# A split-precision decoder trunk: value slabs of the up projections by seven block products, gated products split at the down stage

## The reference, cut to what matters

```python
def conv_ffn(u, w_up, conv_w, conv_b, w_down):
    h = u @ w_up.astype(u.dtype)               # (512,1024) @ (1024,5632)
    h = causal_depthwise_conv(h, conv_w, conv_b)
    gate, val = jnp.split(h, 2, axis=-1)
    return (jax.nn.silu(gate) * val) @ w_down.astype(u.dtype)   # (512,2816) @ (2816,1024)

for i in range(DEPTH):
    ...                                        # mixer of layer i
    f = conv_ffn(rms_norm(x, norm_ffn_pre[i]), ffn_w_up[i], ffn_conv_w[i], ffn_conv_b[i], ffn_w_down[i])
    x = x + rms_norm(f, norm_ffn_post[i])
```

## Time and profile before

| | us |
|---|---|
| median of 3 runs (lowest, highest) | 1138.78 (1138.66, 1138.90) |
| the profiled execution | 1138.84 |
| its span, first to last instruction | 1137.1 |
| granted TensorE clock, mean | 0.999 of full speed |
| busy: TensorE, its weight loads, VectorE, ScalarE, GpSimd | 1127.7, 949.7, 695.5, 524.2, 35.9 |

### The profile page before, as it was taken

The page is one execution under the profiler, slowest core; times in us unless marked ns, Lnnn a source line. Parts: engine busy times, 40 slices in busy tenths (PEclk is TensorE's granted clock), DMA queues, the critical chain, the costliest instruction groups (busy, mean ns, idle before and its releaser), DMA issues.

```text
span 1137.1 us, 14741 instructions
## 1 busy us (share of the span) xinstructions
PE 1127.7 (99%) x5730; PEld 949.7 (84%) x5730; DVE 695.5 (61%) x825; ACT 524.2 (46%) x610; POOL 35.9 (3%) x93
## 2 busy tenths in 40 slices
PE   8999999999999999999999999999999999999998
PEld 7888888888888988888888888899888888888886
DVE  6778889999763865655655321597655565552124
ACT  5667676767533643443443221475443434331213
POOL 6000000000100000000000000000000000000000
PEclk9999999999999999999999999999999999999999
DMA  8244343433233133233233223512232232323221
GB/s 274 76 133 148 121 128 122 133 127 130 75 111 126 61 111 111 79 106 111 74 111 108 98 90 111 167 38 75 93 111 94 91 109 76 110 85 115 96 74 74
DMA packets 85390, 121.74 MB, mean 107 GB/s; under 512 B 4215, under 2 KB 71391, under 8 KB 85344
## 3 DMA queue, kind: packets, MB, share of 16 engines
q1 hardware_dynamic: 85162, 121.02, 32.0%
q10 hardware_dynamic: 182, 0.07, 0.0%
HBM read 118.92 MB, written 2.16 MB: 106 GB/s over the span
## 4 chain that ended last, share of the span: by engine, by line
PE 99%; DMA 1%; ACT 0%; DVE 0%; issue 0%; SPq 0%; DVEq 0%
PE bank L1040 29%; PE bank L307 19%; PE bank L308 19%; PE bank L309 19%; PE bank L515 6%; PE bank L801 1%; PE bank L792 1%; PE bank L753 1%; PE bank L743 1%; PE bank L431 1%; PE bank L1214 1%; DMA raw<-in_ssd_w_in 1%; PE bank L1229 0%; PE bank L1230 0%; PE bank L1231 0%; PE bank L721 0%
## 5 line engine op out<-in xcount | busy, mean ns | idle before, releaser
L307 PE MATMUL bank<-h_hi,w_hi 128*128 128x512 f32 x928 | 364.5, 393 | 0.0
L309 PE MATMUL bank<-h_hi,w_lo 128*128 128x512 f32 x928 | 361.5, 390 | 0.0
L308 PE MATMUL bank<-h_lo,w_hi 128*128 128x512 f32 x928 | 361.2, 389 | 0.0
L277 DVE TENSOR_TENSOR w_lo<-raw,w_hi 128x2048 fp32r<-128x2048 f32 x90 | 206.1, 2289 | 215.0 <-ACT w_hi L272 215.0
L534 DVE SCALAR_TENSOR_TENSOR tmp<-bank,par,tmp 128x511 f32<-128x511 f32 (+2 forms) x248 | 184.9, 747 | 125.3 <-ACT tmp L525 112.4
L272 ACT ACTIVATE w_hi<-raw 128x2048 fp32r<-128x2048 f32 x90 | 171.7, 1908 | 154.0 <-PE bank L1040 152.3
L309 PEld LDWEIGHTS bank<-h_hi,w_lo 128*128 128x128 f32 x928 | 174.2, 188 | 37.1
L307 PEld LDWEIGHTS bank<-h_hi,w_hi 128*128 128x128 f32 x928 | 174.3, 188 | 36.2 <-issue 0.8
L308 PEld LDWEIGHTS bank<-h_lo,w_hi 128*128 128x128 f32 x928 | 174.4, 188 | 35.0
L525 ACT ACTIVATE tmp<-bank,par 128x512 f32<-128x512 f32 x112 | 86.2, 774 | 221.7 <-PE bank L309 201.4
L1040 PE MATMUL bank<-w_lo,act_hi 128*128 128x512 f32 x348 | 107.2, 389 | 0.0
(11 more groups left out here) (203 smaller groups left out, 1030.1 us busy)
## 6 DMA issues: line engine op xcount, KB each, us to landing
raw<-in_ffn_w_up SPq DMA_DIRECT2D x44, 1024.0 KB, 5.0
raw<-in_ffn_w_down SPq DMA_DIRECT2D x22, 1024.0 KB, 4.8
raw<-in_ssd_w_in SPq DMA_DIRECT2D x19, 1024.0 KB, 5.2
decay<-ac_dram SPq DMA_DIRECT2D x16, 512.0 KB, 5.5
raw<-in_ssd_w_out SPq DMA_DIRECT2D x8, 1024.0 KB, 4.8
from_start<-ac_dram SPq DMA_DIRECT2D x32, 128.0 KB, 4.6
xres<-in_x SPq DMA_DIRECT2D x4, 512.0 KB, 6.0
result<-xres SPq DMA_DIRECT2D x3, 512.0 KB, 2.6
```

The source lines that it names most:

```text
L277: dve.tensor_tensor(lo[:], raw[n % 2][:], hi[:].bitcast(F32), ALU.subtract).then_inc(lo_ready, 1)
L307: pe.matmul(dst, wh, xh, start=first, stop=False, **kw)
L308: pe.matmul(dst, wh, xl, start=False, stop=False, **kw)
L309: return pe.matmul(dst, wl, xh, start=False, stop=last, **kw)
```

## The change

The value slabs of passes 2 to 10 of both layers are no longer multiplied as two block products. Slab (1024 x 256) and features (1024 x 512 positions) are cut in two in each direction, and the 2x2 product of these parts is made of seven products of quarters in place of eight (Strassen's scheme in the variant of Winograd): four block weights and seven half-width products of 128 columns by 256 positions, 4 blocks of the contraction x 3 passes each, into halves of banks 0 to 3.

- GpSimd makes, once per layer, the four sums of features (`combos_pool`, ten steps of 128x1024, into `t_new`), which ScalarE and VectorE split into `t_hi`, `t_lo` in pass 1; and in each such pass four sums of weights in place in `raw` (`weights_pool`, four steps of 128x512), which are split by halves into the slot of the pass's own gate slab (`weights_hi_act`, `weights_lo_dve`). The raw slab is released when these are made, not when its own low part is.
- ScalarE copies the first product out of its bank (`first_seven_act`), VectorE assembles the value blocks in `val` in SBUF by four additions (`sevens_dve`); the value taps read `val`.
- The taps and products of the value blocks of pass i are made behind the next value slab's split, at the turn to pass i+1.
- The product gate x value stays in `gated` (float32) and is split two blocks at a time, into `dn_hi`, `dn_lo`, in the down stage; the first pair in pass 4 (`down_hi_act`, `down_lo_dve`).
- The slots of `w_hi`, `w_lo` follow `w_slot`; the first down slab takes chunks 2, 3, 0, 1.
- All loops `Fori` are written out.

```diff
+        def w_slot(n):
+            for l in range(2):
+                i = n - S_UP[l]
+                if 0 <= i < UP_SLABS + DOWN_SLABS:
+                    return (n + max(min(i, UP_SLABS) // 2 - SEVEN0, 0)) % 2
+            return n % 2
-        def load(sp, n, source, view, i=0):
-            if n >= 2:
-                sp.wait_ge(lo_ready, n - 1 + 2 * i)
+        def load(sp, n, source, view):
+            if n >= 2 and seven_of(n - 2) is not None:
+                sp.wait_ge(ws_ready, 2 * seven_of(n - 2) + 2)
+            elif n >= 2:
+                sp.wait_ge(lo_ready, n - 1)
...
+        def seven_product(pe, p, w, x):
+            for k in range(4):
+                mm = three_passes(pe, seven_half(p), w[0][:, k, :], w[1][:, k, :], x[0][:, k, :], x[1][:, k, :],
+                                  k == 0, k == 3)
+            return mm
+        def seven_pe(pe, l, i):
...
+            pe.wait_ge(lo_ready, n + 1)
+            if t:
+                pe.wait_ge(c_ready, t)
+            seven_product(pe, P1, plain(0, 0), h(0, 0))
+            seven_product(pe, P2, plain(0, 1), h(1, 0))
+            pe.wait_ge(t_ready7, 4 * (l + 1))
+            seven_product(pe, P4, plain(1, 1), combo(4)).then_inc(blk_done, 1)
+            pe.wait_ge(ws_ready, 2 * t + 1)
+            seven_product(pe, P7, summed(0, 0), combo(3))
+            seven_product(pe, P5, summed(1, 0), combo(1))
+            pe.wait_ge(ws_ready, 2 * t + 2)
+            seven_product(pe, P6, summed(1, 1), combo(2)).then_inc(p_done, 1)
+            seven_product(pe, P3, summed(0, 1), h(1, 1)).then_inc(blk_done, 1)
...
+        def weights_pool(pool, l, i):
+            n, t = S_UP[l] + 2 * i + 1, SEVENS * l + i - SEVEN0
+            a11, a21, a12, a22 = (quarter(raw[n % 2], m, k) for k in range(2) for m in range(2))
+            pool.wait_ge(lo_ready, n + 1)
+            pool.tensor_tensor(a11, a11, a21, ALU.subtract).then_inc(w_step, 1)
+            pool.wait_ge(w_step, 2 * t + 1)
+            pool.tensor_tensor(a21, a21, a22, ALU.add).then_inc(w_sum, 1)
+            pool.wait_ge(w_sum, 2 * t + 1)
+            pool.tensor_tensor(a22, a22, a11, ALU.subtract).then_inc(w_step, 1)
+            pool.wait_ge(w_step, 2 * t + 2)
+            pool.tensor_tensor(a12, a12, a22, ALU.subtract).then_inc(w_sum, 1)
...
+        def sevens_dve(dve, l, i):
...
+            dve.tensor_tensor(val[:, :, 0, :], both(val[:, 0, 1, :]), seven_pair(P2), ALU.add).then_inc(c_step, 1)
...
+            dve.tensor_tensor(val[:, :, 1, :], both(val[:, 1, 0, :]), seven_pair(P5), ALU.add).then_inc(c_step, 1)
...
+            dve.tensor_tensor(val[:, 1, 0, :], val[:, 1, 1, :], seven_half(P4), ALU.subtract).then_inc(c_step, 1)
...
+            dve.tensor_tensor(val[:, :, 1, :], val[:, :, 1, :], seven_pair(P3), ALU.add).then_inc(c_ready, 1)
...
         def up_act(act, l, i):
...
+            split_hi(act, n + 1, (blk_done, base))
+            if i > SEVEN0:
+                for j in range(2):
+                    up_tap_act(act, l, i - 1, 2 + j)
+            up_tap_act(act, l, i, 0)
+            up_silu_act(act, l, i, 0)
+            if i == SEVEN0 + 2:
+                down_hi_act(act, l, 0)
+            weights_hi_act(act, l, i)
+            up_tap_act(act, l, i, 1)
+            up_silu_act(act, l, i, 1)
+            split_hi(act, n + 2, (blk_done, base + 3))
+            first_seven_act(act, l, i)
...
+        def up_dve(dve, l, i):
...
+            up_taps_dve(dve, l, i, 0)
+            if i == SEVEN0 + 2:
+                down_lo_dve(dve, l, 0)
+            weights_lo_dve(dve, l, i)
+            up_taps_dve(dve, l, i, 1)
+            split_lo(dve, n + 2)
+            sevens_dve(dve, l, i)
+            if i < UP_SLABS // 2 - 1:
+                split_lo(dve, n + 3)
             for j in range(2):
+                up_taps_dve(dve, l, i, 2 + j)
             for j in range(2):
+                up_mul_dve(dve, l, i, j)
```

More of the change, by code:

```diff
@@ L524, in last_tap @@
         def last_tap(act, slot, source, w, b):
-            act.activation(tmp[:, slot, :], bank[:, source, :], ACT.Identity, bias=b, scale=w).then_inc(conv_tap, 1)
+            act.activation(tmp[:, slot, :], source, ACT.Identity, bias=b, scale=w).then_inc(conv_tap, 1)
         def other_taps(dve, count, part, slot, source, weights):
@@ L533, in other_taps @@
                     dve.wait_ge(conv_part, part + j)
-                dve.scalar_tensor_tensor(tmp[:, slot, back:], bank[:, source, 0:T - back], w,
+                dve.scalar_tensor_tensor(tmp[:, slot, back:], source[:, 0:T - back], w,
                                          tmp[:, slot, back:], ALU.mult, ALU.add
@@ L1137, in hybrid_trunk, with quarter, seven_half, seven_pair @@
         PART0 = [2 * CB, 2 * CB + 2 * FB]
-        def up_bank(i, q):
-            return q if isinstance(i, int) and i == 0 else 4 + q
+        P1, P4, P2, P6, P3, P5, P7 = range(7)
+        def quarter(tile, m, k):
+            return by_cols(tile)[:, 4 * k:4 * k + 4, m * P:(m + 1) * P]
+        def seven_half(p):
+            return bank[:, p // 2, (p % 2) * HALF:(p % 2 + 1) * HALF]
+        def seven_pair(p):
+            return bank[:, 0:4, :].rearrange("p b (h n) -> p (b h) n", h=2)[:, p:p + 2, :]
@@ new lines, in h_part @@
+        def h_part(tile, k, half):
+            return tile[:, 4 * k:4 * k + 4, half * HALF:(half + 1) * HALF]
+        def seven_product(pe, p, w, x):
[5 more added lines that the diff above has]
+            n, t = S_UP[l] + 2 * i + 1, SEVENS * l + i - SEVEN0
+            own, other = w_slot(n), 1 - w_slot(n)
+            plain = lambda m, k: [quarter(w[own], m, k) for w in (w_hi, w_lo)]
+            summed = lambda m, k: [quarter(w[other], m, k) for w in (w_hi, w_lo)]
+            h = lambda k, half: [h_part(x, k, half) for x in (h_hi, h_lo)]
+            combo = lambda j: [x[:, j - 1, :, :] for x in (t_hi, t_lo)]
+            pe.wait_ge(lo_ready, n + 1)
[11 more added lines that the diff above has]
+            seven_product(pe, P3, summed(0, 1), h(1, 1)).then_inc(blk_done, 1)
@@ L1142, in up_pe, with up_source @@
+        def up_source(i, q):
+            if i >= SEVEN0 and q >= 2:
+                return val[:, q - 2, :, :].rearrange("p a n -> p (a n)")
+            return bank[:, q if i == 0 else 4 + q, :]
         def up_pe(pe, l, i):
-            for s in range(2):
+            for s in range(2 if i < SEVEN0 else 1):
                 pe.wait_ge(lo_ready, S_UP[l] + s + 1 + 2 * i)
@@ L1177, in up_dve @@
[L1177 to L1185, removed]
-            for j in range(2):
[L1187 to L1195, removed]
@@ new lines, in up_taps_dve, with up_mul_dve @@
+        def up_taps_dve(dve, l, i, q):
+            blk = (q // 2) * FB + q % 2 + 2 * i
+            other_taps(dve, CONV0[l] + q + 4 * i, PART0[l] + q + 4 * i, q, up_source(i, q),
+                       [col("ffn_w", (l * FFN_TAPS + t) * 2 * FB + blk) for t in reversed(range(FFN_TAPS - 1))])
+        def up_mul_dve(dve, l, i, j):
+            dve.wait_ge(gate_silu, FB * l + j + 1 + 2 * i)
+            dve.wait_ge(conv_done, CONV0[l] + 2 + j + 1 + 4 * i)
+            dve.tensor_tensor(gated[:, 2 * i + j, :], tmp[:, j, :], tmp[:, 2 + j, :], ALU.mult).then_inc(u_ready, 1)
@@ L1312, in _ @@
                     sp.dma_start(post_b[:, :], row_of(norm_ffn_post, 1)).then_inc(post_in, 16)
-                with sp.Fori(3, UP_SLABS // 2) as i:
-                    for s in range(2):
-                        up_slab(s, i)
+                for j in range(6, UP_SLABS):
+                    up_slab(j)
                 for s in range(DOWN_SLABS):
@@ L1405, in _ @@
             up_pe(pe, 0, 1)
-            with pe.Fori(2, UP_SLABS // 2) as i:
+            for i in range(2, UP_SLABS // 2):
                 up_pe(pe, 0, i)
@@ L1624, in _ @@
             up_dve(dve, 0, 1)
-            with dve.Fori(2, UP_SLABS // 2) as i:
+            for i in range(2, UP_SLABS // 2):
                 up_dve(dve, 0, i)
             for s in range(1, DOWN_SLABS - 1):
+                down_lo_dve(dve, 0, s)
                 split_lo(dve, S_DOWN[0] + s)
+            down_lo_dve(dve, 0, DOWN_SLABS - 1)
             pool_weights_dve(dve)
@@ L1663, in _ @@
             up_dve(dve, 1, 1)
-            with dve.Fori(2, UP_SLABS // 2) as i:
+            for i in range(2, UP_SLABS // 2):
                 up_dve(dve, 1, i)
             for s in range(1, DOWN_SLABS):
+                down_lo_dve(dve, 1, s)
                 split_lo(dve, S_DOWN[1] + s)
```

265 lines of the change are left out of this document (200 added, 65 removed).

## The result

The changed kernel takes 1210.34 us, median of 4 runs (1210.04 to 1211.45), against 1138.84 for the kernel before (1138.66 to 1139.54, 4 runs): ratio 1.063, 95% interval 1.061 to 1.065, 71.5 us slower. Forecast were 1180 us in a range of 1143 to 1205, so the result lies above it. The direction and the kind of cause held; the size did not, 40.8 us were forecast and 71.5 came. The profiled execution took 1211.45 us, its span is 1209.7, 72.6 more than before.

The account below looks back on a forecast made before the run. TensorE bounds the kernel now; a VectorE-ScalarE loop of 23.5 us would replace its 21.76 us pass. Per layer 13.9 (passes) + 1.0 (pass 4) + 5.5 (opening) = 20.4, two layers +40.8: 1138.84 + 40.8 = 1180 us, range 1143 to 1205.

Parts of the forecast that it names:

- TensorE's part: Up stage, value slab: 84 matmuls of 256 columns at 0.1184 us, 9.94 us for 10.88; TensorE's own pass 20.82 us, 0.94 less.
- the prediction's side sentence: Short matmuls: by the skill's row-group rule weight loads would not be hidden, losing over 260 us; the forecast did not use it.
- The loop: Each seven-product pass: thirteen ordered steps going round between VectorE and ScalarE sum to 21.5 us, without any disturbance.
- GpSimd in the loop: Four weight sums per pass contend with VectorE instructions reading two SBUF tensors: loop 23.5 us taken, bounds 21.5 and 25.
- The price of one entry: GpSimd getting in between two dependent value taps: VectorE waits some 1.1 us each time; one entry gives 22.6, two 23.7.
- no contention: Rival for the passes: GpSimd's sums cost nothing there, loop 21.5 us, kernel 1144 us; chance 0.17.
- Kept out until the products: Branch of the GpSimd term: sums wait until VectorE's value taps and products end at 11.1 us; loop 23.9 us.
- each sum collides: Rival for passes and opening: every weight sum meets VectorE, loop 25, opening +7, kernel 1207 us; chance 0.12.
- The opening: Pass 2 of each layer: late GpSimd feature sums delay the slabs, costing +3.9 to +7.1 us, +5.5 taken.
- Pass 4: Up stage of each layer: ScalarE also splits the first gated pair ahead of the weight sums, +1.0 us.
- The place of TensorE's idle time: Sign: TensorE idle 2 to 3 us per pass before the gate block; longest waits for weight sums would speak against it.
- The down stage: Gated pairs' split moved there, 1.06 us on ScalarE and 1.2 on VectorE, hidden under 10.9 us of matmuls: costs nothing.

## Why the prediction was wrong in size

- **TensorE's part: right.** 256-column matmuls are 0.12 us apart (0.1184 reckoned); a pass of TensorE alone takes 20.98 us (reckoned 20.82). Each has a weight load of its own, and the loads stay hidden, as in the earlier trace rows: by the prediction's side sentence 260 us would have been lost, and they were not. The sentence of the Trainium skill that it went by (TensorE: Matmul & The Clock Gate, "The mechanism": a load overlaps a running matmul only in another row group) does not hold for this stream, and the measurement decides. The same section also says that a load is pulled ahead of running matmuls when it goes into the background weight buffer; the hidden loads agree with that, though no run here shows where they go.
- **The loop: right.** 21.49 us measured without GpSimd, 21.5 reckoned from the earlier trace rows. The waits are those of the written-out pass, not those of the rolled one.
- **GpSimd in the loop: the term that failed.** The prediction took 2.0 us ("Or GpSimd gets in between two dependent taps: ... one such entry ..., two give 23.7"; "I take 23.5"). Measured were 25.43 - 21.49 = 3.94 us. The price of one entry was nearly right: taps and products lost 2.86 and 1.10 us to four sums, 0.99 each (1.1 reckoned). The count was wrong. Behind the plain first tap, GpSimd's four sums got in at four boundaries between VectorE instructions in a row (ahead of taps 2, 3 and 4 and of the first product), each time for about 1 us: four entries, not one or two. One of these boundaries is between the taps of two value blocks, which don't depend on each other. 16 passes x 1.93 = 31 us, and 1180 + 31 = 1211, against 1210.34 measured. That these agree so closely is in part luck: the openings cost 2.8 us less than reckoned, the down stages 2.3 and pass 5 of layer 1 0.9 more. The rows had shown an entry when GpSimd came first and one when VectorE came first; none showed a queue of instructions on both engines, and there the upper bound should have been four. The text itself counted six VectorE instructions with two SBUF inputs at that place, in its case against "no contention".
- **"Kept out until the products"** was the other branch of the same term. It did not happen by itself; the run with one wait more made it happen and gave the prediction's loop, 23.86 for 23.9.
- **The rival "each sum collides"** (loop 25, opening +7, 1207 us, chance 0.12) was nearest. Its loop came out (25.4) though for another reason than it gave: it made each sum 0.15 us longer by its form, but where nothing is in the way that form takes 1.30 (the run with the sums later). The sums took 1.61 to 1.73 because all four entered. Its opening did not come out: +4.0 and +4.2 for +7.
- **The opening: at its lower bound.** +4.0 and +4.2 in a range of 3.9 to 7.1, with 5.5 taken; the last feature sum ended at 433.8, 5 us into pass 2.
- **Pass 4:** +1.1 (26.6 in place of 25.4), +1.0 reckoned.
- **The place of TensorE's idle time: wrong.** The text expected 2 to 3 us ahead of the gate block; 39.9 us in 18 stretches lie ahead of the product that needs the first weight sums, 15.7 in 9 ahead of the gate block. The text named that as a sign against it, which was too strict: the low part of the sums is a step of the same loop (it is VectorE's instruction that releases TensorE in both), and TensorE meets the loop first at the one and then at the other. Another sign stayed out as well: ScalarE waited for GpSimd's last sum only in the two openings (5.0 us in two waits), not in every pass.
- **The down stage: put at nothing, 2.3 us in both together.** The run without seven products is 2.2 us longer than the kernel before.

## What to carry to other kernels

Before giving GpSimd work beside a VectorE chain, look at each VectorE instruction there for two SBUF inputs and count every boundary between such instructions, dependent or not, as an entry for GpSimd while it has work queued, here at about 1 us for a sum of 1.3; a PSUM source for one of the inputs took the price away here (taps 2.97 us in place of 5.83). When TensorE gets faster, add up the loop of the other engines in program order first, since busy shares (VectorE 61%) say nothing about it. Then put what the next stage waits for (slab splits) ahead of what is due later (silus) on ScalarE: here that alone was worth 54 us.

## What was not expected of the hardware

TensorE's granted clock fell in some passes and not in others (mean granted clock of each stretch): 0.93 over the passes 454 to 480, 480 to 506, 532 to 557, 583 to 608 and 634 to 659, and 1.00 over 506 to 532, 557 to 583 and 608 to 634, with the same multiplications in each. Before it fell, TensorE had stood idle for 3.1 us ahead of the gate block at 454.50, for 3.7 us ahead of the first weight sums' product in pass 4, and for 2.6 us there in the later ones; but it stood 2.5 us there in the passes with 1.00 too. In the window shown the clock was 0.54, and matmuls of 256 columns came every 0.21 us. It cost little, as TensorE had slack there: passes of either kind take 25.43 us (pass 4, 480 to 506, takes 1.1 us more, as it does at the full clock in the run without sums). Only in layer 1 did it show: the clock was 0.87 over 904 to 930, the additions at 931.90 waited 0.75 us for the last product of pass 4, and the pass from 930.46 to 956.78 took 26.32 us where it is 25.43 elsewhere.

What decides in which passes the clock falls is open. The run with GpSimd's sums later has 2.6 us of idle time ahead of the gate block in pass after pass; in layer 0 the mean clock was 1.00 over 521 to 546, 0.85 over 546 to 569 and 0.86 over 593 to 617, and in layer 1 it was 1.00 throughout 932 to 1055, with five such waits.
